# Two blocks of linear attention and experts: an exponential ahead of evictions, two casts ahead of the gate, eight weight loads in an earlier stage

## The chip, the cores and the metric

The kernel runs on one core of a Trainium2 chip. The metric is the device time of the whole program in microseconds, lower is better.

## The reference, cut to what matters

The input is 512 grid tokens and 256 context tokens of width 1024. The first block normalises and modulates them, projects them (`z = h @ w_in`), and mixes them in two ways: a gated linear attention with a decay for each channel (GLA, 4 heads with keys of 64 and values of 128, two directions) and a gated delta rule (GDN, 4 heads). A merge gates and adds the two, an output product goes back to the tokens:

```python
def gla_chunked(q, k, v, g, s0):        # g: log decay of each channel
    ...
    bc = jnp.cumsum(gc, axis=3)
    def step(s, inp):
        ...
        diff = bi[:, :, :, None, :] - bi[:, :, None, :, :]
        dec = jnp.exp(jnp.where(causal[:, :, None], diff, -jnp.inf))
        att = jnp.einsum('bhtd,bhsd,bhtsd->bhts', qi, ki, dec)
        ...
# after both mixers
m = sigmoid(gate_a) * (y_a @ w_gla_out) + sigmoid(gate_b) * (y_b @ w_gdn_out)
x = x + g1 * (m @ w_o)
```

A second block (another recurrent mixer, its own merge and output product, and an expert layer, which takes the most time) follows. The diff leaves its code alone but for one semaphore more in its merge.

## The kernel before, in words

The program is a row of stages. A stage is a set of lists of instructions, one for each engine, written out by hand; the engines meet at its end, and SyncE (SP) then clears the stage's semaphores one by one. Inside a stage the only order between engines is that of the waits. Five queues matter: PE (TensorE), ACT (ScalarE), DVE (VectorE), POOL (GpSimd) and SP, which issues the loads.

Three stages bear on the change, and they come one after the other but for the delta rule between the first and the second.

*Linear attention*, `gla_pairs`, two heads at a time (H = 2 pairs). Six weight tiles for each pair (key, query, two of values, two of gates) are projected in float32 accuracy by three products of high and low halves (`product3`, L243 to L245). ACT makes the high half (`high`, L652), DVE the low one (`low`, L785). PE projects in lots of 8 units (384 or 512 columns, three products to a unit) into banks 6 and 7; ACT evicts each lot (`evict`, L662 to L670). PE's list holds the projection as filling: `fill(24)` first (both key lots and the query lot), then 6 or 4 units after each step `at`.

The decay of the scores has no closed product, so the 128 x 128 chunk is cut in seven levels of blocks. For a level `lv` POOL makes two differences of the cumulated decays (L504, L505; ring of DEC = 2 buffers, `dec`, shown as ybT), ACT takes their exponential (L715), DVE multiplies them with keys and queries (`mixed`, L827, L828), PE makes scores (`products`, L561), and DVE keeps those under the level's mask (`kept`, L838 for level 0, L843). POOL starts level i when DVE has multiplied level i - 2. In step `at` PE does `products(at)` and then fills; DVE does `mixed(at)`, `kept(at - 1)`; ACT does the exponential of level `at` and then the copies and evictions of the step:

```python
if at <= LV:
    i = level_of(h, at)
    act.wait_ge(diff_ready, i)
    act.activation(dec..., dec..., ACT.Exp, scale=RATE)...
if at == 2:
    evict(h, V0, 0)
```

PE's level `lv` waits for `mixed(lv)` and, bank by bank, for `kept(lv - 1)`. Before all that come the gates: PE's rate products (L533), ACT's `near` (Abs, L678) and `logs` (Exp and Ln, L682, L683), DVE's `near` (L791) and `scans` (L796 to L809), ACT's `decays` (L689 to L693).

*Merge*, `merge`, 8 iterations: SP loads 1 MB of gate weights (`wg`, one buffer) and 0.5 MB of output weights (`w`, two buffers); ACT casts (L1700), POOL subtracts (L1671), PE makes two gate products of 24 and two plain ones of 4; ACT takes sigmoids, DVE combines (L1721, L1722).

*Output product*, `output_product`: SP issues eight loads of `w_o`, 512 KB each (L1736), PE waits for all of them and makes 8 groups of 8 products (L1745), DVE adds each to the tokens (L1755, L1757).

Of the kernel before, what the change touches and what calls it, by code (L numbers as in the profile page):

```python
# [13 lines left out]
P = 128  # L14
D = 1024
KD = D // P
# [4 lines left out]
NXC = NX // P  # L21
# [5 lines left out]
F32 = mybir.dt.float32  # L27
# [396 lines left out]
def gla_pairs(core, k, hT, alrT, gate, f, dec, yT):  # L424
# [5 lines left out]
    nc, d, ps = core.nc, core.dram, k.ps  # L430
    H, LV, DEC, E = GLA_HEADS // 2, LEVELS, 2, 2
# [6 lines left out]
    with ExitStack() as ctx:  # L438
# [29 lines left out]
        with core.stage("w_in*2", "const_in", "mask_in", "up_clear", "high_ready", "low_ready", "lot_done", "evicted", "up_done",  # L468
# [175 lines left out]
            def _(act):  # L644
                alink = chain(act, asteps)

                def high(n):
                    if n < len(tiles):
                        act.wait_ge(w_in[n % 2], 16 * (n // 2 + 1))
                        if n >= 2:  # L650
                            act.wait_ge(lot_done, first_lot[n - 1])
                        act.copy(wh[:, n % 2, :], w[:, n % 2, :]).then_inc(high_ready, 1)  # L652
# [40 lines left out]
                    act.activation(kds[:, dr], kds[:, dr], ACT.Exp, scale=RATE).then_inc(ce_ready, 1)  # L693

                act.preload_act_table_set("natural_log_exp_and_others")
                act.wait_ge(const_in, 48)
                near(0, 0, 0)
                near(0, 1, 2)
                logs(0)
                high(0)  # L700
                high(1)
                evict(0, K, 0)
                evict(0, K, 1)
                high(2)
# [4 lines left out]
                for h in range(H):  # L709
                    last, n = h + 1 == H, 6 * h  # L710
                    for at in range(1, 2 * LV + 1):
                        if at <= LV:
                            i = level_of(h, at)
                            act.wait_ge(diff_ready, i)
                            act.activation(dec[:, (i - 1) % DEC], dec[:, (i - 1) % DEC], ACT.Exp, scale=RATE).then_inc(dec_ready, 1)  # L715
                        if at == 2:
                            evict(h, V0, 0)
                        if at == 3:
                            evict(h, V0, 1)
                            high(n + G0)  # L720
                        if at in (4, 7):
                            e = 0 if at == 4 else 1
                            if e == 0 and h > 0:
                                act.wait_ge(o_done, h)
                            for c0, c1, b in TURNS:
                                act.wait_ge(vt_done, 4 * h + 2 * e + b - 1)
                                act.copy(vt[:, e, c0:c1, :], ps[:, b, 0:P * (c1 - c0)].rearrange("p (c t) -> p c t", c=c1 - c0)).then_inc(vt_copied, 1)
                        if at == 5:
                            evict(h, V1, 0)
                        if at in (5, 9):  # L730
                            u = 2 * h + (0 if at == 5 else 1)
                            if u > 0:
                                act.wait_ge(u_done, u)
                            for c0, c1, b in TURNS:
                                act.wait_ge(kt_done, 2 * u + b - 1)
                                act.copy(ktok[:, c0:c1, :], ps[:, b, 0:P * (c1 - c0)].rearrange("p (c t) -> p c t", c=c1 - c0)).then_inc(kt_copied, 1)
                        if at == 6:
                            evict(h, V1, 1)
                            high(n + G1)
                        if at == 7:  # L740
                            evict(h, G0)
                        if at == 8:
                            high(n + 6 + K)
                        if at == 9:
                            evict(h, G1)
                            high(n + 6 + Q)
                            if not last:
                                near(h + 1, 0, 0)
                        if at == 10:
                            if not last:  # L750
                                near(h + 1, 1, 0)
                                logs(h + 1)
                            act.preload_act_table_set("sigmoid_and_others")
                            act.wait_ge(evicted, after(h, G1))
                            if h > 0:
                                act.wait_ge(out_done, h)
                            act.activation(scr[:], gate[:], ACT.Sigmoid).then_inc(sig_ready, 1)
                            act.preload_act_table_set("natural_log_exp_and_others")
                        if at == 11:
                            evict(h + 1, K, 0)  # L760
                        if at == 12:
                            if not last:
                                decays(h + 1, 0)
                                decays(h + 1, 1)
                            act.wait_ge(o_done, h + 1)
                            act.wait_ge(gate_ready, h + 1)
                            act.activation(scr[:], ps[:, 4:6, :], ACT.Square).then_inc(sq_ready, 1)
                            evict(h + 1, K, 1)
                        if at == 13:
                            high(n + 6 + V0)  # L770
                        if at == 14:
                            evict(h + 1, Q)
                            high(n + 6 + V1)
                            act.wait_ge(ss_done, h + 1)
                            alink(act.activation(scr[:], ps[:, 4:6, :], ACT.Ln, bias=k.eps[:, 0:1], scale=1.0 / P))
                            act.activation(scr[:], scr[:], ACT.Exp, scale=-0.5).then_inc(rstd_ready, 1)

            @block.vector
            def _(dve):
# [65 lines left out]
                def states(h, dr):  # L845
# [3 lines left out]
                    for i, c in enumerate(ORDER[dr][1:-1], 1):  # L849
# [6 lines left out]
                            ins.then_inc(S_ready, 1)  # L856
                        slot = nxt

                near(0, 0, 0)
                near(0, 1, 2)  # L860
                dve.wait_ge(mask_in, 32)
                dve.wait_ge(const_in, 48)
                scans(0)
                for n in range(3):
                    low(n)
                weighted(0, 0)
                low(3)
                for h in range(H):
# [766 lines left out]
                tail(H - 1)  # L1635


def merge(core, k, hT, w_dram, nA, nB, aT, bT, gate_bias, mT, b_dram=None):

# [4 lines left out]
    with ExitStack() as ctx:  # L1646
# [2 lines left out]
        wh = ctx.enter_context(core.sbuf("mg_wh", [P, 2 * KD, P], F32R))  # L1649
        wl = ctx.enter_context(core.sbuf("mg_wl", [P, 2 * KD, P], F32R))  # L1650
        sg = ctx.enter_context(core.sbuf("mg_sg", [P, 2, 2, NX], F32))
        with core.stage("w_in*2", "g_in", "b_in", "high_ready", "low_ready", "gates_done", "pe_done", "sg_ready", "dsteps", "out_done") as (
                block, w_in, g_in, b_in, high_ready, low_ready, gates_done, pe_done, sg_ready, dsteps, out_done):
            @block.sync
            def _(sp):
                for n in range(KD):
                    if n >= 1:
                        sp.wait_ge(low_ready, n)
                    sp.dma_start(wg[:], w_dram[n][:, nA + nB:width, :]).then_inc(g_in, 16)
                    if n >= 2:  # L1660
                        sp.wait_ge(pe_done, n - 1)
                    sp.dma_start(w[:, n % 2, :, :], w_dram[n][:, 0:nA + nB, :]).then_inc(w_in[n % 2], 16)
                    if n == 0 and b_dram is not None:
                        for g in range(nB // 2):
                            sp.dma_start(bT[:, 2 * g:2 * g + 2, :], b_dram[g]).then_inc(b_in, 16)

            @block.gpsimd
            def _(pool):
# [53 lines left out]
                    dve.tensor_tensor(mT[:, n, :], sg[:, n % 2, 0, :], sg[:, n % 2, 1, :], ALU.add).then_inc(out_done, 1)  # L1722


def output_product(core, k, mT, w_dram, gate_row, alpha, xs):

    nc = core.nc
    ps = k.ps
    with ExitStack() as ctx:
        w = ctx.enter_context(core.sbuf("op_w", [P, KD, D], F32))  # L1730
        y = ctx.enter_context(core.sbuf("op_y", [P, 2, 512], F32))
        with core.stage("w_in", "pe_done", "out_done", "dsteps") as (block, w_in, pe_done, out_done, dsteps):
            @block.sync
            def _(sp):
                for j in range(KD):
                    sp.dma_start(w[:, j, :], w_dram[P * j:P * j + P, :]).then_inc(w_in, 16)  # L1736
                sp.wait_ge(w_in, 16 * KD)

            @block.tensor
            def _(pe):  # L1740
                pe.wait_ge(w_in, 16 * KD)
                for n in range(8):
                    t, h = n // 2, n % 2
                    for j in range(KD):
                        mm = pe.matmul(ps[:, n, :], mT[:, j, P * t:P * t + P], w[:, j, 512 * h:512 * h + 512],  # L1745
                                       start=(j == 0), stop=(j == KD - 1))
                    mm.then_inc(pe_done, 1)
# [95 lines left out]
def first_block(core, k, hT, xs, spare, tap):  # L1843
    nc, d = core.nc, core.dram
    with ExitStack() as ctx:
# [59 lines left out]
        gdn_heads(core, k, hT, gates, b_rows, m1, ybT)  # L1905
        tap("ybT", ybT[:])
        mT = sbt("mT", [P, KD, NX])
        merge(core, k, hT, d["w_merge"], 4, 4, yaT, ybT, b_gate[:], mT)
        tap("mT1", mT[:])
        output_product(core, k, mT, d["w_o"], rows, 1.0, [xs[:, t, :] for t in range(NXC)])  # L1910
        with core.sbuf("final_g", [P, D], F32) as final_g:
            load_all(core, [(final_g[:], d["final_g"].partition_broadcast(P))])
            norm_rows(core, k, [xs[:, t, :] for t in range(NXC)], False, final_g[:], None)
# [1891 lines left out]
```

## Time and profile before

| | us |
|---|---|
| median of three runs (4790.4 to 4795.41) | 4791.02 |
| the profiled execution | 4792.93 |
| its span | 4791.1 |
| linear attention, first block | 197 to 427 |
| merge, first block | 785 to 947 |
| output product, first block | 947 to 1020 |

Over the span PE is busy 83%, DVE 53%, ACT 33%, POOL 18%, at a mean granted TensorE clock of 0.902. Two engines with long idle times are no loss in themselves: what counts is who waited last for whom on the way to PE.

### The profile page before, as it was taken

How to read it: one execution, taken by the hardware profiler on the slowest of the kernel's cores; microseconds unless marked ns; L12 is line 12 of the kernel's file. 1: busy time of each engine (PE TensorE's matmuls, PEld its weight loads, DVE VectorE, ACT ScalarE, POOL GpSimd, SP SyncE). 2: the span in 40 equal slices, each digit the busy share in tenths (PEclk: the TensorE clock that was granted, in tenths of full speed). 3: DMA queues.
4: the chain of work that ended last, by engine and by line, in shares of the span. 5: the costliest groups of instructions: out<-in, count | busy, mean ns of one | idle time of the engine just before them, and what ended most of it. 6: DMA issues, size and time to landing. Idle time of an engine off the chain costs nothing. (4 is left out here: it accounts for less than half of the span.)

```text
span 4791.1 us, 52357 instructions
## 1 busy us (share of the span) xinstructions
PE 3962.1 (83%) x19735; PEld 3261.4 (68%) x19735; DVE 2516.8 (53%) x4208; ACT 1578.8 (33%) x2341; POOL 884.8 (18%) x445
## 2 busy tenths in 40 slices
PE   6387997869488885788886995698979999999995
PEld 5376986538377775677774552586767878888884
DVE  0354773110466663677774003699975555455555
ACT  0333332110344442455554002333653223223322
POOL 0021001100033321111111110242214422222221
PEclk9697999976689897999998997799999999999998
DMA  3011101223111101111112211232656533333331
GB/s 139 31 31 40 32 19 51 91 101 136 36 40 40 37 30 33 40 45 44 41 45 88 88 44 44 94 118 88 200 194 212 189 128 115 117 122 127 116 116 66
DMA packets 134894, 403.46 MB, mean 84 GB/s; under 512 B 16304, under 2 KB 55072, under 8 KB 125088
## 3 DMA queue, kind: packets, MB, share of 16 engines
q1 hardware_dynamic: 134688, 400.68, 24.7%
q8 instruction: 133, 2.18, 0.2%
q14 instruction: 73, 0.60, 0.0%
HBM read 348.18 MB, written 52.45 MB: 84 GB/s over the span
## 5 line engine op out<-in xcount | busy, mean ns | idle before, releaser
L2486 POOL TENSOR_TENSOR ex_vl<-ex_v,ex_vh 128x1024 fp32r<-128x1024 f32 x80 | 192.0, 2400 | 683.2 <-ACT ex_vh L2474 683.2
L243 PE MATMUL ps<-ex_xh,ex_ul 128*128 128x512 f32 x640 | 249.8, 390 | 8.1 <-DVE ex_ul L2493 8.1
L243 PE MATMUL ps<-hT_high,ma_wl 128*128 128x384 f32 (+1 forms) x576 | 233.0, 404 | 25.7 <-DVE ma_wl L3405 25.7
L244 PE MATMUL ps<-ex_xl,ex_uh 128*128 128x512 f32 x640 | 249.4, 390 | 0.0
L245 PE MATMUL ps<-ex_xh,ex_uh 128*128 128x512 f32 x640 | 249.4, 390 | 0.0
L2470 ACT ACTIVATE ex_ab<-ps 128x512 f32<-128x512 f32 x80 | 47.8, 598 | 610.4 <-PE ps L245 610.4
L243 PE MATMUL ps<-ex_vh,ex_al 128*128 128x512 f32 x640 | 249.0, 389 | 0.0
L244 PE MATMUL ps<-ex_vl,ex_ah 128*128 128x512 f32 x640 | 249.0, 389 | 0.0
L245 PE MATMUL ps<-ex_vh,ex_ah 128*128 128x512 f32 x640 | 249.0, 389 | 0.0
L2512 DVE TENSOR_TENSOR ex_acc<-ex_acc,ps 128x512 f32<-128x512 f32 x160 | 109.8, 688 | 248.0 <-PE ps L245 248.0
L1721 DVE TENSOR_TENSOR mg_sg<-mg_sg,ps 128x512 f32<-128x512 f32 x32 | 22.0, 687 | 405.2 <-PE ps L1691 404.6
L2507 DVE TENSOR_TENSOR ex_al<-ex_af,ex_ah 128x512 fp32r<-128x512 f32 x80 | 198.0, 2475 | 61.0 <-ACT ex_ah L2476 61.0
L150 PE MATMUL ps<-cond,mod_w 128*128 128x2 f32 x768 | 164.1, 352 | 70.3 <-DMA mod_w<-in_w_ada_cols 43.5
L2649 POOL TENSOR_TENSOR hg_dec<-hg_cum 128x512 f32<-128x512 f32 x56 | 82.2, 1469 | 730.4 <-DVE hg_cum L2913 577.6
L243 PE MATMUL ps<-hT_high,hg_wl 128*128 128x384 f32 (+1 forms) x512 | 194.2, 379 | 22.1 <-DVE hg_wl L2889 22.1
L150 PEld LDWEIGHTS ps<-cond,mod_w 128*128 128x128 f32 x768 | 164.0, 333 | 71.0 <-issue 71.0
L3101 POOL TENSOR_TENSOR ma_ce<-ma_ce,ma_c 128x512 f32<-128x512 f32 x64 | 94.5, 1477 | 637.2 <-ACT ma_ce L3304 637.2
L245 PE MATMUL ps<-hT_high,ma_wh 128*128 128x384 f32 (+1 forms) x576 | 206.7, 359 | 0.0
L244 PE MATMUL ps<-hT_low,ma_wh 128*128 128x384 f32 (+1 forms) x576 | 206.5, 359 | 0.0
L244 PE MATMUL ps<-hT_low,hg_wh 128*128 128x384 f32 (+1 forms) x512 | 186.8, 365 | 0.0
L245 PE MATMUL ps<-hT_high,hg_wh 128*128 128x384 f32 (+1 forms) x512 | 185.9, 363 | 0.0
L2218 DVE TENSOR_SCALAR sg_two<-iota,chosenT 128x128 f32<-128x128 f32 x512 | 183.9, 418 | 0.0
(509 smaller groups left out, 10735.0 us busy)
## 6 DMA issues: line engine op xcount, KB each, us to landing
ex_u<-in_peer_u SPq DMA_DIRECT2D x80, 512.0 KB, 4.3
ex_v<-in_peer_v SPq DMA_DIRECT2D x80, 512.0 KB, 4.2
gates_by_expert<-sg_gbuf SPq DMA_DIRECT2D x8, 4096.0 KB, 14.8
ma_w<-in_w_in_ma SPq DMA_DIRECT2D x48, 512.0 KB, 3.6
ev_v<-in_peer_v SPq DMA_DIRECT2D x48, 512.0 KB, 3.6
hg_w<-in_w_in_hg SPq DMA_DIRECT2D x40, 512.0 KB, 3.6
ex_g<-gates_by_expert SPq DMA_DIRECT2D x20, 1024.0 KB, 4.8
mg_wg<-in_w_merge SPq DMA_DIRECT2D x16, 1024.0 KB, 5.0
```

The source lines that it names most:

```text
L150: mm = pe.matmul(ps[:, n % 2, 2 * a:2 * a + 2], wt[:, a, k, :], conds[:, k, :], start=(k == 0), stop=(k == KD - 1))
L243: pe.matmul(out, a[1], b[0], start=start, stop=False)
L244: pe.matmul(out, a[0], b[1], start=False, stop=False)
L245: return pe.matmul(out, a[0], b[0], start=False, stop=stop)
L1721: link(dve.tensor_tensor(sg[:, n % 2, a, :], sg[:, n % 2, a, :], ps[:, b + 2 + a, :], ALU.mult))
L2218: ins = dve.tensor_scalar(two[:, t0 + a, :], iota, chosenT[:, 1, t:t + 1], chosenT[:, 2, t:t + 1], ALU.is_equal, ALU.mult)
L2470: act.activation(ab[:, j % 2, :], ps[:, j % 2, :], ACT.Gelu).then_inc(h_read, 1)
L2486: pool.tensor_tensor(vl[:, j], v[:, j % 2], vh[:, j].bitcast(F32), ALU.subtract).then_inc(vl_ready, 1)
L2507: dve.tensor_tensor(al[:, j], af[:, j % 2], ah[:, j].bitcast(F32), ALU.subtract).then_inc(al_ready, 1)
L2512: dve.tensor_tensor(acc[:, n // 2, n % 2, :], acc[:, n // 2, n % 2, :], ps[:, 2 + n % VB, :], ALU.add).then_inc(v_read, 1)
L2649: pool.tensor_tensor(ke, crossed(cums[:, h % 2], size, False, True), crossed(cums[:, h % 2], size, False, False), ALU.subtract)
L3101: pool.tensor_tensor(ce[:, i % 2], ce[:, i % 2], cT[:, P * c:P * c + P].unsqueeze(1).to_broadcast([P, J, P]), ALU.mult).then_inc(ce_scaled, 1)
```

## The change

1. In `gla_pairs` ACT casts the first two weight tiles (`high(0)`, `high(1)`) before the gate's activations and no longer after them. DVE makes their low halves (`low(0)`, `low(1)`) before its own part of the gates and no longer after the scans; `low(2)` stays behind the scans.
2. In `gla_pairs` step 1 of ACT holds the exponentials of levels 1 and 2, and step `at` from 2 to 6 that of level `at + 1`, in front of the evictions and copies of the step.
3. The eight loads of `w_o` in block one are issued by `merge`, into a tensor allocated around both stages; `output_product` doesn't load or wait. Block two's merge and output product keep their loads.

```diff
                 act.preload_act_table_set("natural_log_exp_and_others")
+                high(0)
+                high(1)
                 act.wait_ge(const_in, 48)
                 near(0, 0, 0)
                 near(0, 1, 2)
                 logs(0)
-                high(0)
-                high(1)
                 evict(0, K, 0)
...
-                        if at <= LV:
-                            i = level_of(h, at)
+                        for lv in (1, 2) if at == 1 else (at + 1,) if at < LV else ():
+                            i = level_of(h, lv)
                             act.wait_ge(diff_ready, i)
...
+                low(0)
+                low(1)
+                dve.wait_ge(const_in, 48)
                 near(0, 0, 0)
                 near(0, 1, 2)
                 dve.wait_ge(mask_in, 32)
-                dve.wait_ge(const_in, 48)
                 scans(0)
-                for n in range(3):
-                    low(n)
+                low(2)
                 weighted(0, 0)
...
-def merge(core, k, hT, w_dram, nA, nB, aT, bT, gate_bias, mT, b_dram=None):
+def merge(core, k, hT, w_dram, nA, nB, aT, bT, gate_bias, mT, b_dram=None, after=None):
...
+                    if n >= 2 and after is not None:
+                        for j in range(n - 2, KD if n == KD - 1 else n - 1):
+                            sp.dma_start(after[0][:, j, :], after[1][P * j:P * j + P, :]).then_inc(after_in, 16)
+                if after is not None:
+                    sp.wait_ge(after_in, 16 * KD)
...
-def output_product(core, k, mT, w_dram, gate_row, alpha, xs):
+def output_product(core, k, mT, w_dram, gate_row, alpha, xs, w=None):
...
-                for j in range(KD):
-                    sp.dma_start(w[:, j, :], w_dram[P * j:P * j + P, :]).then_inc(w_in, 16)
-                sp.wait_ge(w_in, 16 * KD)
+                if loads:
+                    for j in range(KD):
+                        sp.dma_start(w[:, j, :], w_dram[P * j:P * j + P, :]).then_inc(w_in, 16)
+                    sp.wait_ge(w_in, 16 * KD)
...
-                pe.wait_ge(w_in, 16 * KD)
+                if loads:
+                    pe.wait_ge(w_in, 16 * KD)
...
-        merge(core, k, hT, d["w_merge"], 4, 4, yaT, ybT, b_gate[:], mT)
-        tap("mT1", mT[:])
-        output_product(core, k, mT, d["w_o"], rows, 1.0, [xs[:, t, :] for t in range(NXC)])
+        with core.sbuf("op_w", [P, KD, D]) as w_o:
+            merge(core, k, hT, d["w_merge"], 4, 4, yaT, ybT, b_gate[:], mT, after=(w_o, d["w_o"]))
+            tap("mT1", mT[:])
+            output_product(core, k, mT, d["w_o"], rows, 1.0, [xs[:, t, :] for t in range(NXC)], w_o)
```

## Rows read from the trace of the kernel before

**Rows 1.** Busy time by stage; columns: stretch, length, engines (instructions), clock, DMA, GB/s.
```profile
197.00:427.00 230.00, 177.80 (x937) 148.41 (x937) 99.46 (x120) 70.75 (x94) 36.65 (x30) 0.81 0.10 30
...
947.00:1020.00 73.00, 57.70 (x128) 25.16 (x128) 11.07 (x16) 0.00 (x0) 0.00 (x0) 0.88 0.15 58
```

**Rows 2.** Waits of 197 to 427: us in total, times, longest.
```profile
PE ps L561 <- DVE gla_att L843: 14.0, 8, 3.4
```

**Rows 3.** Time line at the start of linear attention: start, us, engine, instruction.
```profile
199.02 0.90 SPq L489 DMA_DIRECT2D gla_w<-in_w_in_gla  x2
200.30 5.48 PE L533 MATMUL ps<-smallT,gla_up 32*128 32x384 f32 x8 [12.09 <-DMA gla_up<-in_gla_up]
...
209.65 1.98 ACT L652 CAST gla_wh<-gla_w 128x1024 fp32r<-128x1024 f32 x2
...
217.69 4.09 DVE L785 TENSOR_TENSOR gla_wl<-gla_w,gla_wh 128x1024 fp32r<-128x1024 f32 x2
219.86 0.69 PE L243 MATMUL ps<-hT_high,gla_wl 128*128 128x384 f32 x1 [14.08 <-DVE gla_wl L785]
...
236.25 0.60 ACT L662 ACTIVATE gla_q<-ps 128x512 f32<-128x512 f32 x1 [1.46 <-PE ps L245]
```

**Rows 4.** Time line of levels 3 and 4 in head pair 0.
```profile
245.45 1.16 POOL L505 TENSOR_TENSOR ybT<-gla_cum 128x512 f32<-128x512 f32 x1
...
252.92 1.06 ACT L715 ACTIVATE ybT<-ybT 128x1024 f32<-128x1024 f32 x1
...
255.22 1.32 DVE L843 COPY_PREDICATED gla_att<-gla_mask,ps 128x512 f32<-128x512 uint8 x2
256.00 1.76 PE L561 MATMUL ps<-gla_mix 64*128 64x128 f32 x16 [1.41 <-DVE gla_att L843]
...
264.47 2.50 PE L561 MATMUL ps<-gla_mix 64*128 64x128 f32 x16 [3.40 <-DVE gla_att L843]
264.92 2.10 DVE L785 TENSOR_TENSOR gla_wl<-gla_w,gla_wh 128x1024 fp32r<-128x1024 f32 x1
```

**Rows 5.** TensorE by stretch: length, busy (products), granted clock, DMA; the last four with all engines.
```profile
249.55:285.59 36.04, 28.95 (x184) 0.95 0.05 16
342.20:380.51 38.31, 31.27 (x183) 0.87 0.00 1
285.59:292.29 6.70, 6.70 (x41) 1.00 0.26 78
380.51:388.79 8.28, 8.28 (x40) 0.79 0.01 3
...
200.00:206.00 6.00, 5.48 (x8) 2.47 (x8) 1.02 (x1) 1.08 (x2) 0.00 (x0) 0.50 0.75 259
219.80:224.20 4.40, 4.34 (x14) 4.35 (x15) 1.98 (x1) 0.00 (x0) 2.88 (x2) 0.50 0.59 184
264.50:268.60 4.10, 4.10 (x24) 3.88 (x25) 2.52 (x2) 0.54 (x2) 1.44 (x2) 0.60 0.16 36
960.00:964.60 4.60, 4.60 (x6) 2.00 (x7) 0.00 (x0) 0.00 (x0) 0.00 (x0) 0.50 0.01 4
```

**Rows 6.** Time line of the merge's last gate tile and its end.
```profile
907.45 0.33 SPq L1659 DMA_DIRECT2D mg_wg<-in_w_merge  x1
919.10 1.90 ACT L1700 CAST mg_wh<-mg_wg 128x2048 fp32r<-128x2048 f32 x1 [15.09 <-PE ps L245]
...
945.58 0.69 DVE L1722 TENSOR_TENSOR mT<-mg_sg 128x512 f32<-128x512 f32 x1
947.39 3.76 SPq L1736 DMA_DIRECT2D op_w<-in_w_o  x8
959.96 10.50 PE L1745 MATMUL ps<-op_w,mT 128*128 128x512 f32 x18 [15.93 <-DMA op_w<-in_w_o]
```

**Rows 7.** Loads from issue to landing: the linear attention's tiles, then the merge's.
```profile
DMA to landing us min/median/max: 3.5/3.6/4.6
...
mg_wg<-in_w_merge SPq DMA_DIRECT2D x8, 1024.0 KB, 5.0
```

More of the change, by code:

```diff
@@ L1651, in merge @@
         sg = ctx.enter_context(core.sbuf("mg_sg", [P, 2, 2, NX], F32))
-        with core.stage("w_in*2", "g_in", "b_in", "high_ready", "low_ready", "gates_done", "pe_done", "sg_ready", "dsteps", "out_done") as (
-                block, w_in, g_in, b_in, high_ready, low_ready, gates_done, pe_done, sg_ready, dsteps, out_done):
+        with core.stage("w_in*2", "g_in", "b_in", "high_ready", "low_ready", "gates_done", "pe_done", "sg_ready", "dsteps", "out_done",
+                        "after_in") as (
+                block, w_in, g_in, b_in, high_ready, low_ready, gates_done, pe_done, sg_ready, dsteps, out_done, after_in):
             @block.sync
@@ L1729, in output_product @@
     with ExitStack() as ctx:
-        w = ctx.enter_context(core.sbuf("op_w", [P, KD, D], F32))
+        loads = w is None
+        w = ctx.enter_context(core.sbuf("op_w", [P, KD, D], F32)) if loads else w
         y = ctx.enter_context(core.sbuf("op_y", [P, 2, 512], F32))
```

## The prediction

> **What bounds the kernel now.** I read the stage table first [rows 1], then the waits of the linear attention stage [rows 2], its time line at its start [rows 3] and between two levels [rows 4], the clock by stretch [rows 5], and last the end of the merge [rows 6, 7]. The reader should see in [rows 1] that TensorE (PE) is the busiest engine in linear attention and in the output product, and full in neither: in the first it works 177.8 of 230 us at a mean granted clock of 0.81, in the second 57.7 of 73. So a microsecond counts only if it is one in which PE stands idle or runs at half rate.
>
> Two idle times matter: 14.1 us once, waiting for the low half of the first weight tile [rows 3], and 14.0 us in eight pieces, waiting for VectorE (DVE) to keep the previous level's scores [rows 2]. For the first: the two tiles of weights were requested at 199.02, and such a load takes 3.5 to 4.6 us to land [rows 7], but ScalarE (ACT) casts them only at 209.65, after the gate's four activations, and DVE subtracts only at 217.69, after the scans. PE ends its rate products at 205.78 and starts projecting at 219.86. [rows 4] show the second: ACT's exponential of level 3 starts at 252.92 because the value tile's eviction is in front of it; DVE multiplies after it and keeps level 2 from 255.22, and PE gets level 3 at 256.00. The differences for that exponential were finished by GpSimd (POOL) before 246.61. In [rows 6] PE stands idle for 15.93 us, from the end of the merge to 959.96, for eight loads issued from 947.39 on.
>
> **The change part by part.**
>
> *First weight halves.* Nothing is removed; two casts and two subtractions move ahead. ACT can cast when the tiles are there. By [rows 3, 7] that is 199.02 + 3.5 to 4.6 (the shortest and longest landing of this tile), 202.5 to 204.1 with the second's later issue; a cast is 1.0 us (two in 1.98), a subtraction 1.2 when POOL isn't working (one of the two below took 2.1 beside POOL). The first low half is ready at 204.9 to 206.1, the time at which PE ends its rate products, 205.8. PE starts there: 219.86 - 205.95 = **13.9 us**.
> Does the rest follow? The casts hold ACT until about 205.1, so its first Abs is at 205.2 and not 203.3, but the second had to wait for PE until 205.8 anyway and now starts near 206.1, 0.3 late. DVE reaches its clamps at 206.4, ends them at 208.4, and waits for the logarithms (ACT ends them at 209.65 [rows 3], now at 209.95) as before. The scans and differences end 0.3 us late, at 218.1, and the third low half after them, near 220.2. In the new order PE needs 16.3 us for its three tiles (219.86 to 236.2 before), so the query lot ends at 222.2: the gate chain, once ahead of PE, is now beside it and 2 us early. ACT's six decay activations take 4 us from 217, again before 222. The first exponentials need POOL's differences, finished near 223, and are wanted at 223.9. Two SP loads (tiles 2 and 3) go out at 205 instead of 219.8, behind loads that have landed by then. The cover is thin, 1 to 2 us; if it is gone, the excess is paid one for one.
> The clock: PE ran its first 4.4 us of projection at 0.50, and the rate products at 0.50 throughout [rows 5]. I take no gain there; if the rate products count as a start, up to 2.2 us come back. The Trainium skill, "TensorE: Matmul & The Clock Gate" (Part 1), says that sustained activity of the engine releases its clock, without asking for wide products; if the rate products are such activity, the projection starts at full rate and the time is 2.2 us below my sum. The trace doesn't decide it: the rate products are 5.5 us of work and no release is seen in them.
>
> *Exponential in front.* Work is the same; from level 3 on each exponential stands one step earlier in ACT's queue. It waits there for POOL's differences, which wait for DVE's product two levels back; what is queued behind it on ACT is the eviction of a lot that PE ends later (252.5 against 243.7 for level 3), so nobody is held up. I walked the queues for head pair 0. Level 3: exponential 243.8, product 245.5 (after DVE's keeping of level 1), keeping of level 2 at 250.4, PE free at 254.6 (256.00 - 1.41), no wait. From one level's product to the end of its filling PE takes 5.1 us (256.00 to 264.47 - 3.40), 5.6 with a turn of values, which gives the next times. Level 4: exponential 253.0, product 254.0, keeping 255.3 to 256.7, PE wants it at 259.4. Level 5: exponential 259.7, DVE first has a low half to make (259.7 to 260.9), product to 262.2, keeping to 263.6, PE wants it at 265.2; this is the tightest, 1.6 to 2.3 us. Levels 6 and 7 have 3 us. So all five waits go.
> Price: in head pair 0 PE takes 36.04 us from level 2's product to level 7's, busy 28.95, at clock 0.95 [rows 5]: 7.1 idle and, from 3.6 us at half rate, 1.8 lost. Sum **8.9**. In head pair 1 the same stretch takes 38.31, busy 31.27, clock 0.87: 7.0 idle and some 8.9 busy us at half rate, 4.4 lost; and the stretch after it, level 7 to the updates, takes 8.28 where pair 0 takes 6.70, for its clock of 0.79: 1.6. Sum 13.0. One of its slow pieces (1.7 lost) follows a wait of only 1.41 us and may come back without it, so I take half of it: **12.1**. Together **21.0**; the bounds are 14.1 (idle alone; the clock falls elsewhere) and 21.9. From level 8 on ACT and DVE answer to PE, so the rest only shifts.
>
> *Output weights in the merge.* Eight loads of 512 KB move from the output product to the merge, five behind the tile loads of iterations 2 to 6 and three behind the last, issued near 908 [rows 6]. SP issues each in 0.4 us with nothing behind it before the next low half, 18 us later. Even all 4 MB take 12.6 us alone (947.39 to 959.96); three with the 1.5 MB of tiles land near 919, and the stage ends at 946.3. The wait at the end of SP's list is free. PE then starts where SP started, at 947.4: 959.96 - 947.45 = **12.5**. Clock: the first 4.6 us ran at 0.50 [rows 5], which cost 2.3. PE still stands idle from 944.1 to 947.5, and an idle of 3.4 us in linear attention was followed by 4.1 us at a mean of 0.60 [rows 5], so I take nothing; the bounds are a gain of 2.3 and a loss of 1.0 (a slow stretch as long as the longest in linear attention, some 6.7 us). One more semaphore is cleared after each of the two merges: the merge's 11 are cleared in the 1.12 us between DVE's end and SP's next issue [rows 6], at most 0.1 each, and I take 0.06, **-0.1** in all.
> A rule that speaks against this: the Trainium skill, "DMA: Bandwidth & Descriptors" (Issuing engines are not separate DMA queues), says that all transfers run on the same 16 engines and interleave. Taken at its worst, the added 0.5 MB delays the merge's own loads by its own length, 1.6 us, and they have slack (next part); the sum stays.
>
> Sum: 13.9 + 21.0 + 12.5 - 0.1 = **47.3 us**. The profiled span is 4791.1 and its run took 4792.9, 1.9 over the median of 4791.0. 4792.9 - 47.3 = 4745.6, at the median **4743.7**.
>
> **The rivals.**
> *The waits change their name.* DVE or the clock takes back what the exponentials give: PE still waits for kept scores, since DVE has the low half (2.10 us beside POOL [rows 4]) before level 5's product. For it: 2 us of slack there. Against it: the other levels have 3, and the long wait is level 4's. If that part brings nothing: 4743.7 + 21.0 = 4764.7.
> *The gate chain becomes the bound.* ACT's casts wait for the loads in front of Abs. From a lag of 2 us on, each one delays the first scores. The landing range gives 0.3 to 1.2; 5 us of lag would cost 3, time 4747.
> *The loads aren't hidden.* Some wait on them outlasts the merge, or PE can't start at once: 4743.7 + 12.5 = 4756. Against it: 26 us between landing and end.
> *Slower than before:* the added loads delay the merge's gate tiles. A tile is asked for at 907.45, lands 5.0 later, and is cast at 919.10 [rows 6, 7]: 6.7 us of slack, in each of six iterations. To eat 47 us each must be 6.7 + 8 late, a landing of 20 us against 5. At 22 us the time is 4743.7 + 6 x 10 = 4804.
>
> **How the numbers follow.** The sum's own case 0.82, the waits' new name 0.08, the gate chain 0.04, the loads not hidden 0.04, slower 0.02. Predicted 4744. Low end: clock gains of 2.2, 2.3 and 0.9 give 4738.3; with a microsecond of rounding, 4737. High end: the exponentials at 14.1 give 4751, with a 2 us lag and 1 us of clock at the output 4754, and the case of 4756: 4757. What lies outside is the 0.10 of the first and last rival and little more. A measurement of this kernel tells 0.2%, 9.6 us, from nothing: faster by more 0.97, within it 0.01, slower 0.02.
>
> **What would show it.** PE's first projection product near 206, with the chain of waits no longer naming a low half there. Scores of level 3 to 7 without a wait for DVE, products of level 7 some 27 us after level 2's in both pairs. PE's first output product 3.4 us after its last merge product, still at clock 0.50 for some 4 us. The merge's own iterations 18.15 us apart as before. Wrong would be: ACT waiting for a load past 205, a wait of PE at level 5, a granted clock of 0.50 where there is no idle time, or a gate tile landing after its cast is due.

## The result

| | us |
|---|---|
| before, median | 4792.42 (4790.4 to 4795.41, 4 runs) |
| changed, median | 4737.56 (4735.55 to 4738.75, 4 runs) |
| ratio, 95% interval | 0.9885 (0.9867 to 0.9902) |
| profiled execution, span | 4735.55, 4733.7 |

The kernel is 54.9 us faster at the median. The forecast was 47.3 us less and a time of 4744, its range 4737 to 4757; the measured time lies half a microsecond above the range's lower end. A second comparison, on another occasion (the run e8_again below), gave 4743.53 against 4795.59: 52.1 us, ratio 0.9891 (0.9874 to 0.9907). Its 4743.53 looks like the forecast time only because the kernel before was slower on that occasion too: what can be compared is the difference. So the gain is some 53 us, and the forecast is 5 to 8 us short of it; where these are is the question of this part.

The stages that answer to [rows 1], in the same columns, are these in the changed kernel (linear attention, then output product):

```profile
196.00:387.00 191.00, 167.42 (x938) 139.47 (x938) 99.34 (x120) 71.10 (x94) 36.43 (x30) 0.87 0.12 37
904.00:968.00 64.00, 56.87 (x128) 24.84 (x128) 11.07 (x16) 0.00 (x0) 0.00 (x0) 0.96 0.02 8
```

PE's mean clock rose from 0.81 to 0.87 in linear attention and from 0.88 to 0.96 in the output product (whose stretch before holds the idle time). The two longest waits of PE that are left in linear attention (us in total, times, longest), beside 6.3 us at the change to the next stage:

```profile
PE ps L533 <- DMA gla_up<-in_gla_up: 12.0, 1, 12.0
PE ps L561 <- DVE gla_att L838: 7.3, 2, 4.4
```

The wait of [rows 2] for L843 is gone; that for the keeping of level 0 (L838) was there before with the same 7.3 us. The start of the stage, which answers to [rows 3]:

```profile
197.69 0.90 SPq L489 DMA_DIRECT2D gla_w<-in_w_in_gla  x2
...
198.88 5.48 PE L533 MATMUL ps<-smallT,gla_up 32*128 32x384 f32 x8 [11.98 <-DMA gla_up<-in_gla_up]
...
201.52 1.04 ACT L652 CAST gla_wh<-gla_w 128x1024 fp32r<-128x1024 f32 x1 [3.94 <-DMA gla_w<-in_w_in_gla]
202.60 2.48 DVE L785 TENSOR_TENSOR gla_wl<-gla_w,gla_wh 128x1024 fp32r<-128x1024 f32 x2 [7.26 <-ACT gla_wh L652]
202.77 1.04 ACT L652 CAST gla_wh<-gla_w 128x1024 fp32r<-128x1024 f32 x1 [0.21 <-DMA gla_w<-in_w_in_gla]
...
204.29 0.69 PE L243 MATMUL ps<-hT_high,gla_wl 128*128 128x384 f32 x1
...
220.37 0.60 ACT L662 ACTIVATE gla_q<-ps 128x512 f32<-128x512 f32 x1 [1.44 <-PE ps L245]
```

ACT now waits for the load itself (3.94 us), and the low half is made before PE has ended its rate products: the projection's row carries no wait. Levels 3 and 4, which answer to [rows 4]:

```profile
227.92 1.06 ACT L715 ACTIVATE ybT<-ybT 128x1024 f32<-128x1024 f32 x1 [4.12 <-POOL ybT L505]
236.62 0.48 ACT L666 COPY gla_v<-ps 128x384 f32<-128x384 f32 x1 [7.64 <-PE ps L245]
237.00 1.07 ACT L715 ACTIVATE ybT<-ybT 128x1024 f32<-128x1024 f32 x1
...
229.59 1.69 DVE L827 TENSOR_TENSOR gla_mix<-ybT,gla_k 128x512 f32<-128x512 f32 x1
231.20 0.68 DVE L828 TENSOR_TENSOR gla_mix<-ybT,gla_q 128x512 f32<-128x512 f32 x1
234.83 1.35 DVE L843 COPY_PREDICATED gla_att<-gla_mask,ps 128x512 f32<-128x512 uint8 x2 [2.95 <-PE ps L561]
...
238.70 0.68 DVE L828 TENSOR_TENSOR gla_mix<-ybT,gla_q 128x512 f32<-128x512 f32 x1
239.78 1.36 DVE L843 COPY_PREDICATED gla_att<-gla_mask,ps 128x512 f32<-128x512 uint8 x2 [0.39 <-PE ps L561]
```

The direction of the wait has turned: DVE waits for PE (2.95, 0.39) where PE waited for DVE. The exponential of level 3 starts 8.7 us ahead of the eviction, held only by POOL's differences. TensorE by stretch, which answers to [rows 5] (level 2 to level 7 and level 7 to the updates, for each pair; then the start and the output product):

```profile
233.63:260.40 26.77, 26.77 (x184) 24.37 (x183) 16.39 (x22) 9.36 (x14) 4.63 (x5) 1.00 0.07 21
260.40:267.04 6.64, 6.64 (x41) 5.42 (x40) 1.36 (x3) 2.15 (x4) 0.00 (x0) 1.00 0.25 79
316.52:343.24 26.72, 26.72 (x183) 24.31 (x182) 16.39 (x22) 9.36 (x14) 5.45 (x6) 1.00 0.00 1
343.24:349.89 6.65, 6.65 (x41) 5.43 (x41) 1.36 (x3) 1.45 (x3) 0.00 (x0) 1.00 0.02 4
...
206.00:208.00 2.00, 2.00 (x8) 2.00 (x8) 0.93 (x2) 1.97 (x2) 0.00 (x0) 0.50 0.96 289
208.00:210.00 2.00, 2.00 (x12) 2.00 (x11) 1.47 (x1) 0.44 (x1) 0.00 (x0) 0.90 0.22 90
904.66:907.00 2.34, 2.34 (x3) 1.10 (x4) 0.00 (x0) 0.00 (x0) 0.00 (x0) 0.51 0.02 7
```

Busy equals length at clock 1.00 in both pairs. The end of the merge, which answers to [rows 6]:

```profile
864.61 0.33 SPq L1661 DMA_DIRECT2D mg_wg<-in_w_merge  x1
...
865.46 1.86 SPq L1670 DMA_DIRECT2D op_w<-in_w_o  x3
876.25 1.90 ACT L1707 CAST mg_wh<-mg_wg 128x2048 fp32r<-128x2048 f32 x1 [15.09 <-PE ps L245]
...
902.73 0.69 DVE L1729 TENSOR_TENSOR mT<-mg_sg 128x512 f32<-128x512 f32 x1
904.66 20.82 PE L1755 MATMUL ps<-op_w,mT 128*128 128x512 f32 x44 [3.48 <-PEq L69]
```

The cast of the last gate tile waits for PE, 15.09 us, as before; PE's first output product waits 3.48 us for the change of stage (PEq is PE's own sequencer) and for no load.

Laid side by side by PE's own instructions, the profiled executions differ like this:

| stretch | before | changed | less |
|---|---|---|---|
| first rate product to scores of level 0 | 36.60 | 22.14 | 14.46 |
| level 0 to level 2, pair 0 | 12.65 | 12.61 | 0.04 |
| level 2 to level 7, pair 0 | 36.04 | 26.77 | 9.27 |
| level 7 to scores of level 0, pair 1 | 42.94 | 42.89 | 0.05 |
| level 0 to level 2, pair 1 | 13.67 | 13.23 | 0.44 |
| level 2 to level 7, pair 1 | 38.31 | 26.72 | 11.59 |
| level 7 to the start of the delta rule | 47.2 | 44.3 | 2.9 |
| delta rule | 357.3 | 355.1 | 2.2 |
| merge's first load to first output product | 175.0 | 162.0 | 12.9 |
| first output product to first sum | 9.7 | 8.8 | 0.8 |

The stretches that the diff touches give 52.5 us (14.5 + 21.4 + 2.9 + 12.9 + 0.8); the delta rule's 2.2 and what is left of the 57.4 between the two spans lie in stages that it doesn't touch.

### The profile page after: what moved, and what is told of

Its sections match the earlier page's. It is cut to its first block and busy times, and to the rows that moved or that the text cites. A ratio compares the mean times of both kernels' runs of the same rounds, so it can differ in the third digit from the quotient of the medians.

```text
span 4733.7 us, 52359 instructions
## 1 busy us (share of the span) xinstructions
PE 3948.8 (83%) x19735; PEld 3247.8 (69%) x19735; DVE 2517.5 (53%) x4208; ACT 1578.8 (33%) x2341; POOL 884.5 (19%) x445
## 5 line engine op out<-in xcount | busy, mean ns | idle before, releaser
L2497 POOL TENSOR_TENSOR ex_vl<-ex_v,ex_vh 128x1024 fp32r<-128x1024 f32 x80 | 192.0, 2400 | 684.3 <-ACT ex_vh L2485 684.3
L243 PE MATMUL ps<-hT_high,hg_wl 128*128 128x384 f32 (+1 forms) x512 | 195.9, 383 | 22.5 <-DVE hg_wl L2900 22.5
```

Of the source, the lines that this page charges most:

```text
L243: pe.matmul(out, a[1], b[0], start=start, stop=False)
L2497: pool.tensor_tensor(vl[:, j], v[:, j % 2], vh[:, j].bitcast(F32), ALU.subtract).then_inc(vl_ready, 1)
```

## The experiments

**One part at a time.** Three kernels apply one part of the diff to the kernel before; their edits are the three parts of the diff. The first casts and subtractions alone:

> The kernel before with the first part alone: the first two casts and subtractions ahead of the gates. My theory (the parts add, each counted at the stretch of TensorE that it shortens): from the first rate product to the scores of level 0 22.1 us and no longer 36.6, every later stretch of linear attention as before (36.0 and 38.3 us from level 2 to level 7), time 14.5 us below before, about 4778. Rival (the gains depend on each other: an early start only moves the wait to the levels): the later stretches grow and the gain is under 8 us. A third reading, that the delta rule's 2.2 us came from the earlier stage's order: its stretch is 355.9 here too, and not 358.1.

Measured: 4777.75 against 4793.3 (ratio 0.9969, 0.9958 to 0.998), 15.6 us less. From the first rate product to level 0 it takes 22.7 us. The later stretches keep their waits: 35.75 us from level 2 to 7 in pair 0, 37.37 in pair 1, at clocks of 0.95 and 0.91. The delta rule takes 355.2 us (this expectation and that of the loads set its start 0.85 us earlier, at the first of the gates' products, and so have 355.9 and 358.1 for the table's 355.1 and 357.3). So the gain of this part is its own. The delta rule is shorter here as the third reading said, but it is in the next two kernels as well, whose start is the old one, so that reading falls.

The exponentials alone:

> The kernel before with the exponentials alone moved ahead. My theory: 26.8 us from level 2's scores to level 7's in both pairs of heads, at clock 1.00, 20.9 us less together, 1.6 more behind level 7 of pair 1, and up to 1.7 of clock elsewhere in the stage; the start stays at 36.6. Time 22.5 to 24.2 us below before, about 4769. Rival (the clock falls elsewhere instead, only idle time is won): 14 us, about 4778.

Measured: 4767.34 (ratio 0.9948, 0.9934 to 0.9961), 26.0 us less, 18.7 to 31.6 by the interval; the theory's 22.5 to 24.2 is below the median. The rows of the two pairs and of the stretch behind level 7 of pair 1, in this kernel:

```profile
248.61:275.33 26.72, 26.72 (x183) 1.00 0.07 21
331.40:358.13 26.73, 26.73 (x183) 1.00 0.00 1
358.13:364.80 6.67, 6.67 (x43) 1.00 0.01 4
```

No idle time and no half rate: everything that the stretches had over their pure work is back, not only the idle part. The rival (14 us) is out. By the stage, first rate product to delta rule, it is 227.4 - 202.4 = 25.0 us; 0.6 of it lies before level 0 (36.0 us against 36.6), which this part doesn't touch.

The output weights alone:

> The kernel before with the output weights' loads alone moved into the merge. My theory: the first output product follows the last merge product after 3.5 us and not 15.9, merge iterations 18.15 us apart, first group of the output product 8.8 to 9.7 us: 12.4 to 13.8 us less, about 4779. Rival (the added loads disturb the merge, or the saved wait comes back as half rate): under 10 us. Linear attention and the delta rule must be as before, 226.6 and 358.1 us; if the delta rule is near 356 here, its 2.2 us are chance.

Measured: 4781.60 (0.9974, 0.9965 to 0.9984), 11.7 us less, between 7.7 and 16.8 by the interval. The median is just under the theory's 12.4 to 13.8. By the profile it is 12.9 from the merge's first load to the first output product (175.0 to 162.1), as in the full change, with iterations of 18.2 us as before and a first group of 8.8, and the row says why:

```profile
947.91 12.66 PE L1754 MATMUL ps<-op_w,mT 128*128 128x512 f32 x25 [3.47 <-PEq L69]
```

Linear attention is untouched here, and still its trace differs from that of before: 229.1 us against 227.4, with the clock at 0.87 in pair 0 where it was 0.95, though waits and order are those of before. The delta rule takes 355.2 us. The three parts measured alone sum to 53.3 us, the whole to 54.9 and 52.1: they add.

**Is it the levels' own waits?** In the changed kernel the exponentials of levels 5 to 7 go back to their place:

```diff
-                        for lv in (1, 2) if at == 1 else (at + 1,) if at < LV else ():
+                        for lv in {1: (1, 2), 2: (3,), 3: (4,), 4: ()}.get(at, (at,) if at <= LV else ()):
```

> The changed kernel with the exponentials of levels 5, 6 and 7 in their old place; those of levels 1 to 4 stay ahead. My theory (each level's wait is its own, and the clock falls behind the longer ones): TensorE waits 0.5 us at level 6 and 1.6 us at level 7 in each pair, levels 3 and 4 have none; 4.3 us of idle time more and 0 to 3 us of half rate, time 4.3 to 7 us above the changed kernel, near 4743. Rival (all later levels inherit their lateness from levels 3 and 4): no wait, same time as the changed kernel.

Measured: 4749.57 against 4743.53 for the changed kernel in the same comparison, 6.0 us more. Its scores of levels 5, 6 and 7 in pair 0:

```profile
249.40 1.76 PE L561 MATMUL ps<-gla_mix 64*128 64x128 f32 x16 [0.48 <-DVE gla_att L843]
255.62 1.76 PE L561 MATMUL ps<-gla_mix 64*128 64x128 f32 x16 [0.48 <-DVE gla_att L843]
263.06 1.76 PE L561 MATMUL ps<-gla_mix 64*128 64x128 f32 x16 [1.64 <-DVE gla_att L843]
```

Each level in its old place has a wait again, level 5 too, which I had not expected: it had none in the kernel before, where PE had run at half rate just ahead of it [rows 5] and came later. All six are 5.4 us, and levels 3 and 4 have none, so each wait is its own; the rest of the stage's 8.7 more (197.3 us against 188.6) is clock for the most part: behind level 7 of pair 1 it stands at 0.79 again.

**What does a late load cost at the start?** SP's two constant loads go in front of the first two weight tiles:

```diff
+                sp.dma_start(restart[:], d["restart"][:, 0, :]).then_inc(mask_in, 16)
+                sp.dma_start(mask[:], d["pair_bits"]).then_inc(mask_in, 16)
                 for n, (row, _) in enumerate(tiles):
...
-                    if n == 1:
-                        sp.dma_start(restart[:], d["restart"][:, 0, :]).then_inc(mask_in, 16)
-                        sp.dma_start(mask[:], d["pair_bits"]).then_inc(mask_in, 16)
```

> The changed kernel with SyncE's two constant loads (384 and 112 KB) in front of the first two weight tiles, so that the tiles land later. My theory: the tiles land 1.5 to 2.5 us later, TensorE starts projecting that much later (the start has no slack to its loads), ScalarE's Abs and the gate chain are late by the same and still ready when the query tile ends, so nothing more is lost: 1.5 to 2.5 us above the changed kernel, scores of level 0 at 23.6 to 24.6 us behind the first rate product and not at 22.1. Rival (the gate chain is the bound as soon as it is late): over 4 us.

Measured: 4741.08, no slower than the changed kernel's 4743.53 in the same comparison; its times (4740.39 to 4742.8) overlap with that one's (4740.64 to 4744.85). By the profile it is slower where it was meant to be: the first projection product waits, and level 0 comes 25.1 us after the first rate product and not 22.1, half a microsecond more than the theory's upper bound:

```profile
206.39 0.69 PE L243 MATMUL ps<-hT_high,gla_wl 128*128 128x384 f32 x1 [2.49 <-DVE gla_wl L784]
```

2.5 us of wait, some 0.5 behind it, 0.3 of which is a longer stretch at half rate (4.8 us against 4.1), and no wait of PE for the gate chain. But PE is late together with that chain: the last decay activation ends 1.4 us before the query's eviction here as in the changed kernel. So the run shows that a late load is paid by PE directly; how thin the chain's cover is, it doesn't show. The stage is 192.0 us against 188.6. That the median doesn't show it says how far single medians can be trusted here: in the profiled executions the delta rule, which neither kernel changes, takes 355.1 us against 357.2 and hides 2.1 of the 3.4.

**The waits that are left.** The same cure for level 1. ACT takes the exponential of level 1 before the query's eviction and that of level 2 before its cast (in pair 1 both before the eviction); on DVE the weighting, the fourth low half and the previous pair's last product (`done`) go behind the keeping of level 0:

```diff
                         if at <= LV + 1:
                             kept(h, at - 1)
+                        if at == 1:
+                            weighted(h, 0)
+                            low(n + V1)
+                            if h > 0:
+                                done(h - 1)
...
                 decays(0, 1)
+                grown(0, 1)
                 evict(0, Q)
+                grown(0, 2)
                 high(3)
```

> The changed kernel with the same cure for the waits that are left at level 1: ScalarE takes the exponentials of levels 1 and 2 before the query tile's eviction and cast, VectorE keeps level 0 before it weights the keys, makes the fourth low half and finishes the previous pair. My theory: TensorE's idle 2.9 and 4.4 us before level 1 shrink to under 0.6, so its clock does not fall there (6.8 and 7.2 us at half rate now) and 6 and 7 us are won, about 12 us below the changed kernel, near 4726. Rival (the idle goes, the clock falls all the same): 6 to 7 us, near 4731. Other rival (the work put later becomes the next wait, at level 2 or 3): under 4 us.

Measured: 4730.21 against 4793.3 (ratio 0.9868, 0.9853 to 0.9883), 63.1 us below the kernel before, where the changed kernel was 54.9 and 52.1; 7.3 us below its 4737.56 of another comparison, and 181.5 us against 188.7 in the stage. The idle times before level 1 are 0.29 and 0.26 us, and the clock stays at 1.00 there, but the displaced work is the next wait, at level 2 of either pair:

```profile
229.56 1.76 PE L561 MATMUL ps<-gla_mix 64*128 64x128 f32 x16 [1.07 <-DVE gla_att L851]
308.53 1.76 PE L561 MATMUL ps<-gla_mix 64*128 64x128 f32 x16 [2.15 <-DVE gla_att L851]
```

So the theory was right on the idle times and on the clock, the last rival was right that the work becomes the next wait (3.2 us), and 12 us was too much. One step further, with `if at == 2:` in place of `if at == 1:`:

> As the kernel that keeps level 0 first, but the work put later on VectorE (weighting, fourth low half, the previous pair's last product) goes one step further, behind the keeping of level 1. My theory: the waits of 1.1 and 2.1 us at level 2 go as well, since nothing stands before level 2's product any longer and level 3's is wanted 5 us later; the clock stays at 1.00 from level 0 to level 7. 3 us below that kernel's 4730, 10 us below the changed kernel, near 4727. Rival (the work becomes the next wait at level 3): the same 4730.

Measured: 4732.99 against 4743.53 for the changed kernel in the same comparison, 10.5 us less (ratio to before 0.9872, 0.9856 to 0.9889; the stage is 180.8 us against 188.6). It beats the kernel before and the changed one, but not the kernel with one step less, which stood at 0.9868 to before: the 3 us more that I had expected are missing, and the rival's number is the nearer one, though not for the rival's reason. The waits at level 2 are gone and none came at level 3, but in pair 1 the clock fell, and that stretch takes 3.2 us more than the same one in pair 0, so that the stage is only 0.7 us shorter than with the one step less. The stretches from level 1 to level 2 in pair 0 and, in two pieces, in pair 1:

```profile
223.24:228.23 4.99, 4.99 (x34) 1.00 0.00 0
...
299.92:303.00 3.08, 3.08 (x18) 0.62 0.02 5
303.00:308.06 5.06, 5.06 (x19) 0.56 0.00 0
```

**The changed kernel again.**

> The changed kernel once more, for a second trace and more times. My theory: 4737 again, 55 us below before; linear attention 188.7 us, and the delta rule 355.1 us, which the three kernels with one part each had too, so that the 2.2 us that it differed from the first trace of before were that one execution's. Rival (the first runs were low by chance and the sum of the forecast holds): 4744.

Measured: 4743.53 (4740.64 to 4744.85) against 4795.59 (4789.55 to 4799.15). Linear attention 188.6 us, both stretches of levels 26.85 and 26.83 at clock 1.00. The time is the rival's 4744, the 52.1 us less are nearer to the theory's 55 than to the forecast's 47. The delta rule takes 357.2 us this time and not 355.1: the same kernel has 355.1 and 357.2, and the three kernels with one part each, of old and new order, have 355.0 to 355.2. Its 2.2 us in the first pair of traces are chance.

## Why the prediction was right, and what it missed

The traces of the runs, sorted by the order that each kernel has in the stretch in question, show how much of a difference is chance:

| stretch | old order | new order |
|---|---|---|
| first rate product to scores of level 0 (first casts) | 36.60, 36.02, 35.92 | 22.67, 22.14, 21.94 |
| scores of level 0 to the delta rule (exponentials) | 190.8, 190.9, 193.2 | 166.4, 166.5, 166.7 |
| PE idle before the first output product (loads) | 15.93, 16.79, 16.52 | 3.47, 3.48, 3.47 |

The old order is that of the kernel before and of the two one-part kernels that leave the stretch alone; the new one that of the kernel with this part alone, of the changed kernel and of e8_again.

*First weight halves, 13.9.* Right, 14.5 in the first pair of traces and 13.9 by the means of the table, so that the 0.6 over the forecast is chance. PE's first projection product moved from 19.56 to 5.41 us behind the first rate product, which is 14.15. The cast started 3.83 us after the request and not up to 4.6, so the low half was ready before PE wanted it. Most of the rest is the stretch at half rate: 4.1 us where it had been 4.5. The zero taken for the clock stands: PE ran 3.6 to 5.2 us of projection at 0.50 in six traces with the early start, and 3.3 to 4.5 us in the three with the late one, so 5.5 us of rate products just ahead bought nothing that these traces show. The Trainium skill's rule ("TensorE: Matmul & The Clock Gate", Part 1), that sustained activity releases the clock, was weighed ahead as a possible 2.2 us; for the rate products no run here shows it. The gate chain beside PE was in time as walked: the last decay activation ended at 218.9, 1.4 us before the query's eviction.

*Exponentials, 21.0.* The mechanism was right to 0.2 us: in the time of the kernel before, the exponentials of levels 3 and 4 were walked at 243.8 and 253.0; the scores of level 0 now come 15.9 us sooner (236.90 and 221.02), which makes 227.9 and 237.1, and the rows have 227.92 and 237.00. No wait came at level 5, the tightest, whose low half ran alone (1.22 us and not 2.1). "All five waits" was a slip: each pair had four that count, at levels 3, 4, 6 and 7. The size was the term that failed most: 24.3 us from level 0 on in the first pair of traces. It was worked out as idle time plus half-rate time between levels 2 and 7, with half of one slow piece left in; measured are 9.27 + 11.59 + 1.6 = 22.5 us there (8.9 + 12.1 forecast), above all because the slow piece that followed a wait of 1.41 us went with the wait. Outside the stretches that I summed 1.2 us lie behind the last level of pair 1: between the updates and the delta rule PE has the same idle time in both kernels (11.6 us), and the clock fell 0.9 us ahead of the products of scores with values (L629) before and 1.6 us into them now. The stretch from the updates to the delta rule, before and changed:

```profile
388.79:427.72 38.93, 27.32 (x122) 0.62 0.00 0
...
349.89:387.57 37.68, 26.07 (x122) 0.66 0.00 0
```

The last 0.5 us, between levels 0 and 2, are chance: pair 1 took 13.67 us before, but 13.30 and 13.29 in e1_halves and e3_loads with the same order. The price was read from one trace, and this was a kind one: the stretch from level 7 of pair 0 to pair 1 took 42.9 us in it and 44.6 in the two others of the old order, and level 2 to 7 of pair 0 took 36.0, 35.8 and 38.3. By the means of the table the part is worth 25.1 us. The rival that the clock takes the gain back is refuted by e2_exp.

*Output weights, 12.5.* Right, 12.45 for the wait itself (15.93 to 3.48), and 12.9 by the means: the loads' last landing scatters too. The merge up to its last product and the first group of the output product ran 0.5 and 0.8 us shorter. For the most part that isn't the loads' doing, since e1_halves and e2_exp, which have the old loads, are as short in the merge (158.7 and 158.6 us, 159.1 before) and show 9.0 and 9.1 us for the first group where before has 9.7. The slower rival needed gate tiles landing after 20 us; the last four casts of gate tiles all wait 15.09 us for PE, as before. The Trainium skill's rule ("DMA: Bandwidth & Descriptors", Issuing engines are not separate DMA queues), that all transfers share the same 16 engines and interleave, costs nothing here: the added loads took 7.5 us to land in the median, where the same loads took 6.5, 7.4 and 7.1 in the three traces of the old place; nobody waited for them.

*The sum.* By stretches 52.5 us against 47.3: 0.6 at the start, 3.3 in the exponentials (1.5 in the stretches, 1.8 outside), 1.4 at the merge and the output product. The rest of the 54.9 is the scatter of the untouched stages, which move by 2 us from one execution to the next. By the means of the table it is 13.9 + 25.1 + 12.9 = 51.9 us, and what the forecast lacks is then the exponentials' 4 us almost alone. That the time still lies in the range is in part luck: its lower end was made of gains of clock at the first projection and at the output product (2.2 and 2.3), of which the means show 0.4 at most, and it was the exponentials that filled the room.

What stays open: why the clock fell in pair 1 of e5_level0b, and whether block two's output weights would bring the same 12 us, which wasn't tried. Where the waits go is shown by the runs; why the clock falls behind some of them and not behind others isn't.

## What to carry to other kernels

An engine that has several kinds of work in one list should do first what the bottleneck's next step hangs on, even if it must wait for its input there, as long as nothing behind it is wanted sooner. A short wait before each burst of the matrix engine costs more than its own length when the clock falls behind it: price such a wait as idle time plus half of the time at half rate in the stretch, look beyond the stretch, and take the price from more than one trace. Work that is put later needs a place with slack of its own; one step too early it is only the next wait.

## What the runs showed of the hardware

- Five and a half microseconds of products with 32 rows, back to back, left the granted clock at 0.50. It rose after 3.6 to 5.2 us of full products right behind them (six traces), no sooner than after an idle time of 14 us (3.3 to 4.5 us, three traces).
- The clock can fall while PE is working. In e5_level0b PE stood idle for 0.73 us before level 0 and 0.26 us before level 1 of pair 1 and ran the next 8.1 us at 0.62 and 0.56, while pair 0, after 0.69 and 0.29 us, stayed at 1.00, and so did pair 1 of e4_level0 after 0.73 and 0.26.
- The same wait doesn't always bring the same fall. After 1.63 to 1.64 us before level 7 of pair 0 the clock fell to 0.50 for 3.4 us in e1_halves and e3_loads (44.6 us to pair 1), and stayed at 1.00 in the kernel before and in e6_exp34 (42.9 us).
- The same instructions in the same order, with the same waits, gave 227.4 and 229.1 us of linear attention in two kernels, and the delta rule 355.1 and 357.2 us in two executions of one kernel. It is the clock's doing where the stretches show it (0.95 and 0.87 in pair 0; 0.966 and 0.963 in the delta rule, which is some half of its difference).
